# A mixture-of-experts block: residual, normalisation and store moved from a combine stage into every expert tile, up product 512 wide

## What is computed

```python
a = silu(ragged_dot(xs, w_gate, sizes)) * ragged_dot(xs, w_up, sizes)
ys = ragged_dot(a, w_down, sizes) * weight
out = zeros_like(xt).at[tok_s].add(ys)
h = layernorm(alpha * h1 + out, ln2_g, ln2_b)
```

## Time and profile before

| | us |
|---|---|
| median of 3 runs | 4585.82 (4583.0 to 4588.31) |
| span of the profiled execution | 4592.1 |
| experts, from the first gate product to the last down product | 1499.7 |
| combine, to the end of the span | 266.9 |

### The profile page before, as it was taken

The page is one execution under the profiler, slowest core; times in us unless marked ns, Lnnn a source line. Parts: engine busy times, 40 slices in busy tenths (PEclk is TensorE's granted clock), DMA queues, the critical chain, the costliest instruction groups (busy, mean ns, idle before and its releaser), DMA issues. The chain is left out here.

```text
span 4592.1 us, 68431 instructions
## 1 busy us (share of the span) xinstructions
PE 4189.9 (91%) x22196; PEld 3537.4 (77%) x22197; DVE 2398.3 (52%) x3696; ACT 1641.4 (36%) x2767; POOL 789.1 (17%) x741
## 2 busy tenths in 40 slices
PE   7999999999999999999999976999999999999600
PEld 7887887887887887887878865888888888888500
DVE  5554455455445445445445556554444555444477
ACT  2423323323323223224224222554444555444311
POOL 4022022022012112111210202000000000000266
PEclk9999999999999999999999987999999999999855
DMA  6233233233333332333332314774444565345377
GB/s 163 70 106 96 79 103 95 88 97 88 92 97 86 98 94 83 101 84 92 102 91 84 103 58 152 264 283 170 173 164 164 217 231 192 141 176 212 128 265 242
DMA packets 560688, 622.93 MB, mean 136 GB/s; under 512 B 90048, under 2 KB 412608, under 8 KB 560464
## 3 DMA queue, kind: packets, MB, share of 16 engines
q1 hardware_dynamic: 536992, 534.56, 35.7%
q0 software_dynamic: 23472, 85.47, 5.6%
HBM read 532.92 MB, written 87.03 MB: 135 GB/s over the span
## 5 line engine op out<-in xcount | busy, mean ns | idle before, releaser
L809 PE MATMUL bank<-hT_hi,w_hi 128*128 128x512 f32 x2176 | 869.2, 399 | 42.0 <-DVE w_lo L645 33.3
L810 PE MATMUL bank<-hT_lo,w_hi 128*128 128x512 f32 x2176 | 853.5, 392 | 3.9 <-issue 3.9
L811 PE MATMUL bank<-hT_hi,w_lo 128*128 128x512 f32 x2176 | 851.9, 391 | 0.0
L645 DVE TENSOR_TENSOR w_lo<-raw,w_hi 128x1024 fp32r<-128x1024 f32 x400 | 545.0, 1363 | 505.7 <-ACT w_hi L506 504.5
L1388 DVE TENSOR_TENSOR e_w_lo<-e_raw,e_w_hi 128x1024 fp32r<-128x1024 f32 x384 | 455.0, 1219 | 346.5 <-ACT e_w_hi L1346 343.3
L1443 PE MATMUL e_bank<-e_w_hi,e_xT_hi 128*128 128x256 f32 (+1 forms) x1968 | 627.1, 319 | 1.5 <-DVE e_xT_lo L1383 1.5
L1445 PE MATMUL e_bank<-e_w_hi,e_xT_lo 128*128 128x256 f32 (+1 forms) x1968 | 627.4, 319 | 0.0
L1444 PE MATMUL e_bank<-e_w_lo,e_xT_hi 128*128 128x256 f32 (+1 forms) x1968 | 627.2, 319 | 0.0
L809 PEld LDWEIGHTS bank<-hT_hi,w_hi 128*128 128x128 f32 x2176 | 410.7, 189 | 158.3 <-issue 41.6
L810 PEld LDWEIGHTS bank<-hT_lo,w_hi 128*128 128x128 f32 x2176 | 411.1, 189 | 88.0 <-issue 6.8
L811 PEld LDWEIGHTS bank<-hT_hi,w_lo 128*128 128x128 f32 x2176 | 410.5, 189 | 88.3
(11 more groups left out here) (251 smaller groups left out, 6703.2 us busy)
## 6 DMA issues: line engine op xcount, KB each, us to landing
raw<-in_w_in_dram SPq DMA_DIRECT2D x251, 512.0 KB, 3.9
e_raw<-in_w_exp_gate_dram SPq DMA_DIRECT2D x128, 512.0 KB, 4.3
e_raw<-in_w_exp_up_dram SPq DMA_DIRECT2D x128, 512.0 KB
e_raw<-in_w_exp_down_dram SPq DMA_DIRECT2D x128, 512.0 KB, 11.4
expert_rows<-e_y SPq DMA_DIRECT2D x82, 512.0 KB, 2.8
raw<-in_w_o_dram SPq DMA_DIRECT2D x64, 512.0 KB, 3.8
h_rows<-h_rows SPq DMA_DIRECT2D x36, 512.0 KB, 3.1
raw<-in_w_in_dram SPq DMA_DIRECT2D x64, 256.0 KB, 3.8
```

Of the source, the lines that this page charges most:

```text
L645: v.tensor_tensor(w_lo[:, s % 2, :], raw[:, s % RAW, :], w_hi[:, s % 2, :].bitcast(FP32), ALU.subtract).then_inc(lo_ready, 1)
L809: pe.matmul(out, hi, x_hi, start=first, stop=False)
L810: pe.matmul(out, hi, x_lo, start=False, stop=False)
L811: return pe.matmul(out, lo, x_hi, start=False, stop=last)
```

## The change

The combine stage and the buffer `ys` are gone. `h1` is stored twice by the mixer, one copy behind the other. Every expert tile gathers its input from the first copy. Of a frame's two expert rows, the one in the earlier tile also takes its base from the first copy, adds its weighted result and writes the sum to the second (the part scatter); the one in the later tile takes its base from the second copy, adds its own result, normalises and writes the row of `out` (the row scatter). Both scatters are issued for every tile, with the indices of rows that don't belong to them out of bounds. The weights are divided by `alpha` and the epsilon by its square, so that `h1` needn't be scaled. The router lists four indices and a weight per slot; ScalarE scales the one-hot tables by index and weight, and the small matmul is 196 columns wide instead of 98. The up product is one of 512 columns in bank 1; the transposes of the next rows come ahead of those of the product. VectorE adds weight times result to the base out of the banks and takes the statistics; GpSimd makes the deviation, ScalarE normalises, GpSimd multiplies by the gain, adds the shift and stores. SP only loads.

```diff
@@ mixer, SP @@
-                            sp.dma_start(h1[bass.ds(b * TOK + i1 * P, P), :], h[:, i1, :]).then_inc(h1_out[i1], 16)
+                            for at in (0, TOK + S):
+                                sp.dma_start(h1[bass.ds(b * TOK + (at + i1 * P), P), :], h[:, i1, :])\
+                                  .then_inc(h1_out[i1], 16)
...
@@ mixer, GpSimd @@
-                        hold(po, h1_out[i1], 16 * b + 16)
+                        hold(po, h1_out[i1], 32 * b + 32)
...
@@ route, ScalarE @@
+                for j in range(2 * NT):
+                    if j % 3:
+                        a.wait_ge(hi_made_dve, j - j // 3)
+                    else:
+                        a.wait_ge(hi_made, j // 3 + 1)
+                    if j >= OH:
+                        a.wait_ge(hots_used, j - OH + 1)
+                    for q in range(2):
+                        ins = a.activation(listed[:, j % OH, q, :], hot_hi[:, j % OH, :], ACT.Copy,
+                                           scale=worth[:, j, q:q + 1])
+                    ins.then_inc(worth_made, 1)
...
@@ route, TensorE @@
-                    mm = pe.matmul(ranks[0][:, 0:MT], hot_lo[:, j % OH, :], hot_hi[:, j % OH, :],
+                    pe.wait_ge(worth_made, j + 1)
+                    mm = pe.matmul(ranks[0][:, 0:2 * MT], hot_lo[:, j % OH, :],
+                                   listed[:, j % OH, :, :].rearrange("p q t -> p (q t)"),
                                    start=(j == 0), stop=(j == 2 * NT - 1))
...
@@ experts, SP @@
                     for c in range(CH):
                         hold(sp, *split_count(e, c, False))
                         load(e + 1, c)
-                    stores(e)
-                stores(E - 1)
...
@@ experts, GpSimd @@
+                def gather_rows(g):
                     hold(po, t_ready, g * 2 + 2)
+                    po.tensor_copy(x_at[:, :], row_index[:, bass.ds(g, 1), 0]).then_inc(x_at_set, 1)
+                    hold(po, x_at_set, g + 1)
+                    po.indirect_dma_start(out=rows[:, :], out_offset=None, in_=h1[0:TOK + S, :],
+                                          in_offset=bass.IndirectOffsetOnAxis(ap=x_at[:, 0:1], axis=0))\
                       .then_inc(rows_in, 16)
                     hold(po, rows_in, g * 16 + 16)
+                def gather_base(g):
+                    po.tensor_copy(y_at[:, :], row_index[:, bass.ds(g, 1), 1:3].rearrange("p o q -> p (o q)"))\
+                      .then_inc(y_at_set, 1)
+                    hold(po, y_at_set, g + 1)
+                    po.indirect_dma_start(out=base[:, :], out_offset=None, in_=h1[:, :],
+                                          in_offset=bass.IndirectOffsetOnAxis(ap=y_at[:, 0:1], axis=0))\
+                      .then_inc(base_in, 16)
+                def store_part(g):
+                    hold(po, y_taken, g * 2 + 4)
+                    po.indirect_dma_start(out=h1[:, :],
+                                          out_offset=bass.IndirectOffsetOnAxis(ap=y_at[:, 1:2], axis=0),
+                                          in_=both[:, :], in_offset=None,
+                                          bounds_check=h1.shape[0] - 1, oob_is_err=False).then_inc(part_out, 16)
+                def deviation(g):
+                    po.tensor_copy(out_at[:, :], row_index[:, bass.ds(g, 1), 3]).then_inc(out_at_set, 1)
+                    hold(po, moments_made, g + 1)
+                    po.tensor_scalar(rstd[:, :], moments[:, 1:2], LN_EPS / (ALPHA * ALPHA), None, ALU.add)\
+                      .then_inc(rstd_made, 1)
+                    hold(po, rstd_made, g * 3 + 1)
+                    po.tensor_tensor(rstd[:, :], rstd[:, :], minus_half[:, :], ALU.pow).then_inc(rstd_made, 1)
+                    hold(po, rstd_made, g * 3 + 2)
+                    po.tensor_scalar(offset[:, :], moments[:, 0:1], rstd[:, 0:1], -1.0, ALU.mult, ALU.mult)\
+                      .then_inc(rstd_made, 1)
+                def store_rows(g):
+                    hold(po, normed, g + 2)
+                    po.tensor_tensor(done[:, :], done[:, :], gain[:, :], ALU.mult).then_inc(gained, 1)
+                    hold(po, gained, g * 2 + 1)
+                    po.tensor_tensor(done[:, :], done[:, :], shift[:, :], ALU.add).then_inc(gained, 1)
+                    hold(po, gained, g * 2 + 2)
+                    hold(po, out_at_set, g + 1)
+                    po.indirect_dma_start(out=out[:, :],
+                                          out_offset=bass.IndirectOffsetOnAxis(ap=out_at[:, 0:1], axis=0),
+                                          in_=done[:, :], in_offset=None,
+                                          bounds_check=S - 1, oob_is_err=False).then_inc(rows_out, 16)
+                    hold(po, rows_out, g * 16 + 16)
+                gather_rows(0)
+                gather_base(0)
+                gather_rows(1)
+                with po.Fori(0, total) as g:
+                    gather_rows(g + 2)
+                    store_part(g)
+                    deviation(g)
+                    hold(po, part_out, g * 16 + 16)
+                    gather_base(g + 1)
+                    store_rows(g)
...
@@ experts, ScalarE, end of a tile @@
-                        a.wait_ge(y_ready, g * 2 + 3)
-                        a.wait_ge(y_out, g * 16 + 16)
-                        a.activation(y[:, 0:TOK], yp[0][:, :], ACT.Copy).then_inc(y_taken, 1)
+                        a.wait_ge(rstd_made, g * 3 + 3)
+                        a.activation(done[:, :], both[:, :], ACT.Identity, bias=offset[:, 0:1], scale=rstd[:, 0:1])\
+                         .then_inc(normed, 1)
...
@@ experts, VectorE @@
-                        splits((0, 1), (0, 1))
+                        splits((0, 1, 2), (0, 1, 2))
                         v.wait_ge(act_ready, g + 2)
+                        v.wait_ge(up_ready, g + 1)
+                        for j in range(KF):
+                            part = slice(j * P, (j + 1) * P)
+                            v.tensor_tensor(prod[:, part], up_p[:, part], act[:, part], ALU.mult)\
+                             .then_inc(prod_ready, 1)
...
                         splits((), range(GC, 2 * GC))
-                        v.tensor_copy(y[:, TOK:2 * TOK], yp[1][:, :]).then_inc(y_taken, 1)
+                        v.wait_ge(base_in, g * 16 + 16)
+                        v.wait_ge(normed, g + 1)
+                        for half in range(2):
+                            v.wait_ge(y_ready, g * 2 + 3 + half)
+                            part = slice(half * TOK, (half + 1) * TOK)
+                            v.scalar_tensor_tensor(out=both[:, part], in0=yp[half][:, :],
+                                                   scalar=slot_weight[:, bass.ds(g, 1)], in1=base[:, part],
+                                                   op0=ALU.mult, op1=ALU.add).then_inc(y_taken, 1)
+                        for half in range(2):
+                            v.wait_ge(y_taken, g * 2 + 3 + half)
+                            ins = v.bn_stats(stats[:, half, :], both[:, half * TOK:(half + 1) * TOK])
+                        ins.then_inc(stats_made, 1)
+                        hold(v, stats_made, g + 1)
+                        v.bn_aggr(moments[:, :], stats[:, :, :]).then_inc(moments_made, 1)
...
@@ experts, TensorE @@
-                        for part, (out, c0, ready) in enumerate(((gate_p, 0, gate_ready), (up_p[0], GC, up_ready),
-                                                                 (up_p[1], GC, up_ready))):
+                        for out_p, c0, ready in ((gate_p, 0, gate_ready), (up_p, GC, up_ready)):
+                            if c0 == 0:
+                                pe.wait_ge(act_ready, g + 1)
...
+                        transposes(g * 16 + 32)
                         product_transposed(0)
                         product_transposed(1)
-                        transposes(g * 16 + 32)
                         product_transposed(2)
```

More of the change, by code:

```diff
@@ L26 @@
 BOTH = 1024
+NOWHERE = 65536.0
 def hold(eng, sem, value):
@@ L470, in _ @@
                     sp.wait_ge(ln_done, BLOCKS * LNS + i1 + 1)
[L471 to L472 removed]
+                    for at in (0, TOK + S):
+                        row = at + BLOCKS * TOK + i1 * P
+                        sp.dma_start(h1[row:row + P, :], h[:, i1, :]).then_inc(h1_out[i1], 16)
                 for i1 in range(TILES):
[L474 removed]
+                    sp.wait_ge(h1_out[i1], 32 * (BLOCKS + 1))
             @block.gpsimd
@@ L986, in route @@
     L = G + E
-    slot1, slot2, weight1, weight2, slot_token, bounds, slot_tiles = keep
+    row_index, slot_weight, bounds, slot_tiles = keep
     MT = slot_tiles
+    SECOND = TOK + NT * P
     with ExitStack() as ctx:
@@ L1125, in _ @@
                 link(v.tensor_tensor(weight2[:, :], weight1[:, :], gap_exp[:, :], ALU.mult))
+                link(v.tensor_tensor(later[:, :], tied1[:, :], tied2[:, :], ALU.is_lt))
```

(46 more changed lines are left out.)

249 lines of the change are left out of this document (55 added, 194 removed).

## The result

The changed kernel takes 4916.38 us (median of 4 runs, 4912.31 to 4919.01) against 4586.14 (4 runs on the same chip, 4583.0 to 4588.31): a ratio of 1.072, 95% interval 1.071 to 1.074. The forecast was 4886 in a range of 4550 to 5110. The profiled execution spans 4910.6 us.

What follows compares the result with a forecast made beforehand. GpSimd's strict-order iteration, 24.9 us with three DMA waits in place, was to set the pace over TensorE's 18.7. 2850 + 82 x 24.9 gave a span of 4892, less 6 for the runs: 4886 us, range 4550 to 5110.

Steps and rivals of the forecast that it cites:

- The sum: Whole kernel: first part scatter at 2855, then 81 iterations and the end, a span of 2850 + 82c, 4892 us.
- c: Length of one iteration in the expert stage, forecast at 24.9 us; the span breaks even at 21.2.
- GpSimd's iteration: Expert stage: GpSimd works in strict order, waits in place for three DMAs and sets the pace at 24.9 us; chance 0.68.
- my choice between the bounds: Landing of GpSimd's scatters: 4.3 us, the quiet gather, taken between 2.8 (direct store) and 7.8 (slow gather).
- The floor of the other loop: Scatter through deviation, Silu, splits and down product to next scatter: 22.0 us first tile, 21.3 last, 18.7 elsewhere, mean 21.
- rival 3: Extra transfers and GpSimd's multiplications disturb weight loads and VectorE: iteration 28 us or more, time over 5140; chance 0.08.
- Rival 1: GpSimd stays under the pace; ScalarE's wait for the deviation decides, iteration at the floor of 21, 4566 us; chance 0.15.
- Rival 2: The deviation comes so early that no tile has a hole; every tile takes 18.7 us, 4385 in all; chance 0.09.
- The up product: TensorE, each tile: 512-wide matmuls save 0.31 us, transposes no longer overlapped cost 0.87, so 18.16 becomes 18.7 us.
- The start of the experts: Routing stage: ScalarE's scaled copies, small operations and the mixer's last stores delay the experts by 8 us.
- The lower clock after a hole: TensorE after a wait runs at 1.2 instead of 2.4 GHz; the down product takes 8.4 us instead of 5.7.
- Holes "in nearly all tiles": Sign of being right: TensorE stands between row transposes and products' transposes in nearly all tiles, down products at low clock.

Runs made afterwards that it cites:

- no_gain: The changed kernel without GpSimd's two operations, the gain multiplication and shift addition, that part of the result left uncomputed: 4641.5 us.
- late_norm: dve_norm_halves with VectorE's two normalising instructions of a tile moved behind the next tile's products: 4469.3 us, ratio 0.975 to the kernel before.
- early_waits: The changed kernel with GpSimd no longer waiting in place for the row gather, and waiting for the row scatter one iteration later: 4839.8 us.
- dve_norm: early_waits with normalising, gain and shift as two VectorE instructions right behind the statistics, none of it on ScalarE or GpSimd: 4553.2 us.
- dve_norm_halves: dve_norm with the up product back in two halves of 256 and the products' transposes ahead of the rows': 4492.8 us.
- late_spare: late_norm with two more 128x1024 GpSimd multiplications per iteration, into a tile that nothing reads: 4591.8 us, ratio 1.001 to the kernel before.

## Why the prediction was right, and where it was not

**The sum.** 2850 + 82c held: the first part scatter is at 2858.3 (forecast 2855), and c is 25.05 for 24.9. Of the 30 us that are missing, 3 are at the start, 12 are the 0.15 us of 81 iterations, 3 lie behind the last part scatter (23.4 us for 20.3), and 12 are the difference between span and run: I took 6 off, and it came out as 6 more (4910.6 against 4916.4).

**GpSimd's iteration.** Its mechanism was right, and so was its size on average: by the trace GpSimd's own order takes 24.4 us for 24.9. It is not the same in all tiles. In the plain tile shown every part is shorter than forecast: the part scatter to the issued base gather takes 5.6 us for 6.2, gain and shift 4.9 for 6.0, the row scatter with its landing 4.2 for 5.1, the gather with its own 6.6 for 7.6: 21.4 for 24.9. In the first tile shown it is 7.1, 5.7, 5.6 and 8.3, some 26.6 in all. The scatters land in 3.3 and 2.7 us in the plain tile, near the direct store (2.8) and not the gather (4.3), which was my choice between the bounds; a landing under 3 us was one of the signs of being wrong, and in the plain tiles it came. Over the stage the row scatters' median is 4.3 and the part scatters' 3.2.

**The step that failed.** The floor of the other loop, "22.0 in the first tile of an expert (32), 21.3 in the last (30)", was 26.1 and 26.5, and it decided in 41 tiles of 81. In the tile shown the terms are: to Silu 6.5 for 5.5, splits to products 7.9 for 4.1, the down product 7.95 for 8.4, the end 2.0 for 1.8. The mis-sized term is VectorE's splits: three at 1.2 us each by the rows of before, where GpSimd did nothing beside them. The forecast priced GpSimd's multiplications only as time of GpSimd; what they do to VectorE stood in rival 3 alone, with 0.08 and "over 5140". The total was helped by luck: against the forecast's 24.9 the 20 plain tiles are 3.9 us shorter (79 us together), the 61 others 1.5 longer on average (91). Some 40 of those 91 are GpSimd's own order, which is longer there than in the plain tiles: shift takes 3.1 us beside the splits, and the gathered rows land in 5.1 to 5.6 us on average for 4.4. The rest is the loop that lies above it. So the forecast named one of two orders of nearly equal length, and the one that ends last in 40 tiles of 81.

**The rivals.** Rival 1 (GpSimd under the pace, c at the floor) came true in part: the loop behind ScalarE's wait for the deviation decides in 41 tiles of 81. But GpSimd is not at 21 or under, and its time, 4566, did not come, because the floor was wrong too; no_gain, where the splits are short, is at 4641.5. What was held against it, that the gather took "4.2 or more in all 83 cases", was misread: the shortest is 4.0. Rival 2 (4385) wanted the expert boundary to cost nothing. Even late_norm doesn't get there. Rival 3 had the right disturbance, of VectorE by GpSimd's multiplications, and too high a price for it. Of the Trainium skill's fit for one DMA (DMA: Bandwidth & Descriptors, Anatomy of one DMA), 2.6 us for half a tile is near what the row scatter of the plain tile took (2.7), and under the medians of the stage. Its 3.2 for 512 KB was too short: no gather of the changed kernel landed under 4.1.

**The smaller steps.** The up product was forecast to cost 0.56 us a tile without a hole: 18.73 against 18.16 measured. The start of the experts was +8, measured +8.6. The second store of h1 cost nothing that can be seen: the first instruction of routing comes 4 us earlier than before (2743.0 for 2746.8), so the routing stage itself takes some 12 us more. Neither was tried alone. The lower clock after a hole was as forecast, 7.95 us for 8.4. Holes "in nearly all tiles" were not: TensorE waits for the products in 61 tiles of 82, and in the plain ones it goes from gate product to gate product in 18.73 us without that wait; what GpSimd is late there comes out, by the order of the program, in the Silu of a tile behind.

**What the 330 us are.** Removing gain and shift from GpSimd gives back 275 us, with GpSimd's waits and Silu's order also changed 441. Of the combine stage's 266.9 us 241 were gained; the expert stage grew by 551.

## What to carry to other kernels

Before moving elementwise work to an idle engine, ask which engine's instructions it will lie beside, and not only how long it takes: with gain and shift on the idle GpSimd (early_waits) the kernel took 287 us more than with them on VectorE (dve_norm). Split a stage by kind of tile before comparing a mean with a forecast, and work out how long each order would take alone: where two are nearly equal, undoing one gives back little. A fusion that removes a stage pays only if what it adds finds room in the loop: here it took 7% more time as written, 2.0% less in dve_norm_halves, and 2.5% less with the normalising one tile later.

## What the runs showed of the hardware

VectorE's 128x1024 split of two tiles in SBUF took 1.22 us alone and up to 3.4 us in the change, 4.3 in late_spare, beside GpSimd's 128x1024 operations on two tiles in SBUF; those took 2.4 us, and up to 3.4 beside VectorE. The three splits of the first tile shown (min/median/max ns) are

```profile
L1469 DVE TENSOR_TENSOR e_w_lo<-e_raw,e_w_hi x3: 1212/2436/3359, 3410.3 to 3415.9; 128x1024 fp32r<-128x1024 f32 x3
```

The one of 2,436 comes first, beside the end of gain, the one of 3,359 beside shift, and the one of 1,212 last, beside nothing. In that tile the rest of gain (1.35 us), shift at its undisturbed length (2.4) and the three splits at theirs (3.50) add up to some 7.2 us, and the splits took 6.86: the two engines hardly overlapped. The Trainium skill (SBUF — State Buffer, SBUF: two separate sides) says that VectorE and GpSimd share a pair of ports, which the one that starts first holds for its whole instruction when VectorE has two inputs in SBUF and GpSimd reads SBUF; the trace agrees nearly.

A 128x1024 subtraction and multiplication in one took VectorE 1.28 us, where ScalarE's normalising took 1.24 and each of GpSimd's two operations 2.3 or more.

An indirect write landed in 2.7 us in the plain tile shown and in 2.1 at the least, with a median over the stage of 3.2 for the part scatters and 4.3 for the row scatters; the indirect gathers of 512 KB took 4.1 to 9.0, median 5.1 for the rows and 4.4 for the base.
